# Order of work in a fused two-block transformer kernel: modulation sums, first transfers and one feed-forward seam

## The reference, cut to what matters

```python
# first block
mod = silu(c) @ w_ada + b_ada                     # 1024 -> 6 x 1024
shift1, scale1, gate1, shift2, scale2, gate2 = split(mod, 6)
h = rms_norm(x, g_norm1) * (1 + scale1) + shift1
proj = h @ w_in                                   # and so on: attention, w_out, w_up, w_down
# second block, layer 0
mem_n = rms_norm(mem, mem_norm_g)                 # a memory of 256 rows
mkv   = mem_n @ a_mem_kv                          # keys and values; layer 1 has b_mem_kv
...
x = x + concat([y_mix, m]) @ a_w_out              # "a_out" in the kernel
x = x + swiglu(rms_norm(x, a_norm2_g), a_ffn_gu, a_ffn_down)    # "a_gu", "a_down"
```

## Time and profile before

| | |
|---|---|
| median of 3 runs | 1088.08 us (1087.13 to 1091.59) |
| the profiled execution | 1086.01 us, of it span 1084.2 us |
| PE busy | 1037.8 us (96% of the span) |
| DVE busy | 740.6 us (68%) |
| ACT busy | 553.7 us (51%) |
| DMA | 185.88 MB, mean 171 GB/s |

### The profile page before, as it was taken

One profiled execution on the slowest core, in us unless ns is written; L12 is line 12 of the kernel. 1 busy time (PEld: TensorE's weight loads), 2 busy tenths in 40 slices (PEclk: granted clock), 3 DMA queues, 4 the chain that ended last, 5 costly groups with the idle time before them and its releaser, 6 DMA issues.

```text
span 1084.2 us, 23734 instructions
## 1 busy us (share of the span) xinstructions
PE 1037.8 (96%) x10388; PEld 986.5 (91%) x10388; DVE 740.6 (68%) x1216; ACT 553.7 (51%) x836; POOL 0.9 (0%) x7
## 2 busy tenths in 40 slices
PE   7999999899999999999798999999999999999996
PEld 6888889899999998886678999999998799999996
DVE  4799758799976667888456555566757755566554
ACT  5426354666556458755135444444667655444531
POOL 0000000000000000000000000000000000000000
PEclk8999999999999999999999999999999999999998
DMA  9958455466645653331004555456323445554451
GB/s 370 382 191 310 177 207 194 156 234 233 233 141 185 221 224 117 118 117 44 5 2 156 195 194 190 139 165 211 129 77 115 183 152 187 184 181 154 168 177 40
DMA packets 30664, 185.88 MB, mean 171 GB/s; under 512 B 3408, under 2 KB 4704, under 8 KB 13408
## 3 DMA queue, kind: packets, MB, share of 16 engines
q1 hardware_dynamic: 30560, 184.36, 47.1%
HBM read 183.29 MB, written 1.05 MB: 170 GB/s over the span
## 4 chain that ended last, share of the span: by engine, by line
PE 88%; DVE 6%; ACT 3%; DMA 1%; issue 1%; SPq 0%; DVEq 0%; ACTq 0%
PE banks L359 47%; PE banks L1338 17%; PE banks L339 5%; PE banks L356 2%; DVE wlo L319 1%; PE banks L630 1%; ACT whi L304 1%; PE banks L633 1%; DMA raw<-in_ada 1%; PE banks L568 1%; PE banks L1860 1%; PE banks L1877 1%; PE banks L1870 1%; PE banks L1522 1%; DVE adac L552 1%
## 5 line engine op out<-in xcount | busy, mean ns | idle before, releaser
L319 DVE TENSOR_TENSOR wlo<-raw,whi 128x2048 fp32r<-128x2048 f32 (+3 forms) x163 | 323.1, 1983 | 173.6 <-ACT whi L304 172.8
L304 ACT ACTIVATE whi<-raw 128x2048 fp32r<-128x2048 f32 (+3 forms) x163 | 270.7, 1662 | 121.6 <-PE banks L1338 76.8
L359 PE MATMUL banks<-h_hi,whi 128*128 128x256 f32 x1376 | 182.7, 284 | 1.3 <-ACT h_hi L980 1.2
L359 PE MATMUL banks<-h_lo,whi 128*128 128x256 f32 x1376 | 178.5, 281 | 0.7 <-DVE h_lo L1052 0.7
L359 PE MATMUL banks<-h_hi,wlo 128*128 128x256 f32 x1376 | 178.3, 281 | 0.0
L359 PEld LDWEIGHTS banks<-h_hi,whi 128*128 128x128 f32 x1376 | 170.4, 190 | 5.1 <-issue 2.8
L359 PEld LDWEIGHTS banks<-h_lo,whi 128*128 128x128 f32 x1376 | 167.2, 187 | 3.5 <-issue 1.8
L359 PEld LDWEIGHTS banks<-h_hi,wlo 128*128 128x128 f32 x1376 | 168.5, 189 | 1.5 <-issue 1.0
L1364 ACT ACTIVATE u<-u 128x256 f32<-128x256 f32 x44 | 18.4, 418 | 128.9 <-DVE u L1418 128.8
L1338 PE MATMUL banks<-m_lo,whi 128*128 128x256 f32 x528 | 75.0, 280 | 0.0
L1338 PE MATMUL banks<-m_hi,whi 128*128 128x256 f32 x528 | 74.9, 280 | 0.0
(11 more groups left out here) (448 smaller groups left out, 1394.0 us busy)
## 6 DMA issues: line engine op xcount, KB each, us to landing
raw<-in_ada SPq DMA_DIRECT2D x24, 1024.0 KB, 5.3
raw<-in_w_up SPq DMA_DIRECT2D x22, 1024.0 KB, 4.8
raw<-in_a_gu SPq DMA_DIRECT2D x22, 1024.0 KB, 4.8
raw<-in_b_gu SPq DMA_DIRECT2D x22, 1024.0 KB, 4.8
raw<-in_w_in SPq DMA_DIRECT2D x12, 1024.0 KB, 6.1
raw<-in_w_down SPq DMA_DIRECT2D x16, 704.0 KB, 4.1
raw<-in_a_in SPq DMA_DIRECT2D x11, 1024.0 KB, 5.6
raw<-in_a_down SPq DMA_DIRECT2D x16, 704.0 KB, 4.1
```

Source lines behind the costliest of these rows:

```text
L304: act.activation(hi_s[k % NSPLIT][:, 0:w], raw[n % NRAW][:, 0:w], ACT.Copy).then_inc(*hi_made.tick(k))
L319: dve.tensor_tensor(lo_s[s][:, 0:w], raw[n % NRAW][:, 0:w], hi_s[s][:, 0:w].bitcast(F), SUB).then_inc(*lo_made.tick(k))
L359: i_ = pe.matmul(b[0:m, j * T:(j + 1) * T], a[:, kt * step + j * m:kt * step + j * m + m], x[:, kt, :], start=st, stop=sp)
```

## The change

In the prologue: `mem` and the first memory weights are each loaded by one transfer instead of two halves, and the first memory product goes through its sixteen products by output half, with one wait for its weights. The second memory weights are issued ahead of X instead of behind it. PE's sums of modulation chunks stand one to three pieces later among the memory products, so do the two means with the column; the sums of 6 and 7 stand together ahead of the last piece. `pe_wake` runs seven products instead of five.

At the seam: ScalarE and VectorE make the splits of `a_gu` 0 and 1 ahead of squares 2 and 3 or between them, squares 4 to 7 come behind the gains, and the split of `a_gu` 2 is last on both.

```diff
-        d_mem, d_wfg = [sig(f"landed_mem{i}", 16) for i in range(2)], sig("landed_wfg", 16)
-        d_mkv = [[sig(f"landed_mkv{i}_{n}", 16) for n in range(2 if i == 0 else 1)] for i in range(4)]
+        d_mem, d_wfg = sig("landed_mem", 16), sig("landed_wfg", 16)
+        d_mkv = [sig(f"landed_mkv{i}", 16) for i in range(4)]
...
         def act_mem_gain(act):
             for kt in range(8):
-                if kt % 4 == 0:
-                    act.wait_ge(*d_mem[kt // 4].at(0))
...
             w, b = mkv_w[c], bank[c % 2]
-            halves = [range(0, 4), range(4, 8)] if c == 0 else [range(8)]
-            turns = [(n, j, kt) for n, half in enumerate(halves) for j in range(2) for kt in half]
-            for o, (n, j, kt) in enumerate(turns):
-                if j == 0 and kt == halves[n][0]:
-                    pe.wait_ge(*d_mkv[c][n].at(0))
+            pe.wait_ge(*d_mkv[c].at(0))
+            for o, (j, kt) in enumerate(itertools.product(range(2), range(8))):
...
             act.preload_act_table_set(LN_EXP)
+            act.wait_ge(*d_mem.at(0))
             act_mem_gain(act)
...
-        EARLY_SUMS = {(0, 2): 0, (1, 0): 1, (1, 3): 2, (2, 1): 3, (2, 3): 4, (3, 0): 5, (3, 2): 6, (3, 3): 7}
+        EARLY_SUMS = {(0, 3): (0,), (1, 1): (1,), (2, 0): (2,), (2, 2): (3,), (3, 0): (4,), (3, 1): (5,), (3, 2): (6, 7)}
...
-            if c == 0 and piece == 3:
+            if c == 1 and piece == 0:
                 pe.wait_ge(*d_con0.at(0))
                 pe_mean8(pe, "mem", bank[5])
-            if c == 1 and piece == 1:
+            if c == 1 and piece == 3:
                 pe_mean8(pe, "n1", bank[6])
                 pe_rs_column(pe)
-            if (c, piece) in EARLY_SUMS:
-                pe_ada(pe, EARLY_SUMS[c, piece])
+            for i in EARLY_SUMS.get((c, piece), ()):
+                pe_ada(pe, i)
...
-            for n in range(5):
+            for n in range(7):
                 pe.matmul(bank[0][:, 0:T], rmask[:, 0:P], rmask[:, 0:T], start=True, stop=True)
...
         def act_residual_a(act):
-            for f in range(6):
-                act.wait_ge(*x_made.at(("a_out", f)))
-                act_square(act, "a_out", f, X[:, f, :])
+            def squares(*fs):
+                for f in fs:
+                    act.wait_ge(*x_made.at(("a_out", f)))
+                    act_square(act, "a_out", f, X[:, f, :])
+
+            squares(0, 1)
             act_split(act, split_k["a_out", 1] + 3)
             act_split(act, split_k["a_out", 2] + 3)
+            squares(2, 3)
             act.wait_ge(*done_at("a_out", 3))
             for kt in range(8):
                 act_gain1(act, "nf2", kt, X, V("a_g2", 0, 8), x_made.at(("a_out", kt)))
-            for f in (6, 7):
-                act.wait_ge(*x_made.at(("a_out", f)))
-                act_square(act, "a_out", f, X[:, f, :])
+            squares(4, 5, 6, 7)
             act_split(act, split_k["a_out", 3] + 3)
...
         def dve_residual_a(dve):
-            for i in range(4):
+            def tiles(i):
                 dve.wait_ge(*done_at("a_out", i))
                 for j in range(2):
                     f = 2 * i + j
                     dve.tensor_tensor(X[:, f, :], res_bank("a_out", i)[:, j * T:j * T + T], X[:, f, :],
                                       ADD).then_inc(*x_made.tick(("a_out", f)))
-                if i == 0:
-                    dve_square(dve, "a_out", 1)
-                if i == 2:
-                    for f in range(2, 6):
-                        dve_square(dve, "a_out", f)
-                    dve_split(dve, split_k["a_out", 1] + 3)
+
+            tiles(0)
+            dve_square(dve, "a_out", 1)
+            tiles(1)
+            tiles(2)
+            dve_split(dve, split_k["a_out", 1] + 3)
+            dve_square(dve, "a_out", 2)
+            dve_square(dve, "a_out", 3)
+            dve_split(dve, split_k["a_out", 2] + 3)
+            tiles(3)
             for kt in range(8):
                 dve_gain1(dve, "nf2", kt, X, V("a_g2", 0, 8))
-            dve_square(dve, "a_out", 6)
-            dve_split(dve, split_k["a_out", 2] + 3)
+            for f in (4, 5, 6):
+                dve_square(dve, "a_out", f)
             dve_split(dve, split_k["a_out", 3] + 3)
...
                 if n == 0:
-                    for h in range(2):
-                        t4, c4 = slice(4 * h, 4 * h + 4), slice(1024 * h, 1024 * h + 1024)
-                        sp.dma_start(mem[:, t4, :], A["memT"][:, t4, :]).then_inc(*d_mem[h].tick(0))
-                        sp.dma_start(mkv_w[0][:, c4], A["mkv_a"][0][:, c4]).then_inc(*d_mkv[0][h].tick(0))
+                    sp.dma_start(mem[:, :, :], A["memT"]).then_inc(*d_mem.tick(0))
+                    sp_mkv(sp, 0)
                 if n == 2:
                     sp.dma_start(con[:, 0:NFIRST], A["cons"][:, 0:NFIRST]).then_inc(*d_con0.tick(0))
+                    sp_mkv(sp, 1)
                     sp.dma_start(X[:, :, :], A["xT"]).then_inc(*d_x.tick(0))
-                    sp_mkv(sp, 1)
```

More of the change, by code:

```diff
@@ L1 @@
+import itertools
 import math
@@ L3200, in sp_mkv @@
             name, i = ONE[c]
-            sp.dma_start(mkv_w[c], A[name][i]).then_inc(*d_mkv[c][0].tick(0))
+            sp.dma_start(mkv_w[c], A[name][i]).then_inc(*d_mkv[c].tick(0))
         def sp_program(sp):
```

## The result

The changed kernel takes 1085.48 us (median of 12 runs, 1082.51 to 1088.76), the kernel before 1088.51 us (12 runs beside it, 1086.71 to 1092.45): ratio 0.9972 [0.9959, 0.9985], so 3.0 us faster, which is less than 0.5%. The forecast was 1084.5 us. In a second set it took 1086.71 us, ratio 0.9984 [0.9968, 1.0]. (A ratio compares runs side by side, so it is not exactly the quotient of the medians.)

A forecast was written before the change was run, and what follows sets the result against it. TensorE, busy 96% of the span, was taken as the bound, so gains come only from its waits or low clock. Prologue 2.1 + seam 1.5 = 3.6 us off the median of 1088.08 gave 1084.5 us, range 1081.8 to 1088.8.

The forecast's parts named there:

- S, the first memory product: Prologue: PE's first memory product starts at 9.8 (ends 9.3 and 10.5), before 7.94, costing PE 1.4 to 2.6 us.
- S + 17.5 to the column: Prologue: PE runs without waiting for sum 0, so VectorE's copy of the column comes at 27.3, before at 28.34.
- From the column 18.1 us to mod (16.9 + 1.2): Prologue: VectorE works 16.9 us to chunk 7's end, then 1.2 to its mod row: 45.4 if the clock holds.
- this cap: Prologue: arrival of modulation weights allows mod at 45.2 at old rates, so DMA caps the gain at about 4 us.
- The clock falls at the start and costs 1.65, mod at 47.1: Prologue, forecast case: PE idles 2.8 us before the first memory product and the clock falls; chance 0.46.
- clock holds: Rival, prologue start: idle may be the old 1.80 us; gain 3.8 + 1.5, so 1082.8 us; chance 0.22.
- The rule weighed there: Prologue start: the skill says idle gaps over about 3 us drop the clock; at the seam 2.78 us was enough.
- The gain at mod: 2.1: Prologue: VectorE's mod at 47.1 instead of 49.18, a gain of 2.1 us.
- The seam: 0.69 us, then 2.0 us of new wait, gain 1.5: From a_out to a_gu: PE starts 2.1 us sooner, then waits 2.0 for square 6; means at 587.3, before 588.86.
- The chance of 0.45 for a fall in the new wait: Seam: PE's new wait ahead of the means may drop the clock in any case, adding 1.65 us; chance 0.45.
- The total: Whole kernel: 2.1 + 1.5 = 3.6 us gained, giving 1084.5 us.
- I count what mod gains as kept: After the prologue: w_in steps start from mod or a weight slot they free, so mod's gain is kept.

The follow-up runs named there:

- halves: The changed kernel with mem and the first memory weights loaded in halves again, first product in half-turns: 1088.71 us, ratio to before 0.9987.
- prologue only: The changed kernel with the seam's order of before (old residual functions): 1086.26 us, ratio to the kernel before 0.9964.
- wake of five: The changed kernel with five products of ones in pe_wake instead of seven: 1087.06 us, ratio to the kernel before 0.9977.
- X first: The changed kernel with X issued ahead of the second memory weights again: 1089.03 us, ratio to the kernel before 0.9999.
- after: The whole changed kernel against the kernel before: 1085.48 us, ratio 0.9972; in a second set 1086.71 us, 0.9984.
- seam once more: Repeat of the kernel before with the seam's new order alone: 1088.59 us, ratio to the kernel before 1.0002.
- means covered: The changed kernel with the second feed-forward's means behind two of six pieces of a_gu chunk 1: 1082.77 us, ratio to before 0.9946.
- seam only: The kernel before with the new order of the seam alone: 1088.87 us, ratio to the kernel before 1.0002.
- ones at the seam: The kernel before with six unused products of ones behind chunk 3 of a_out: 1088.59 us, ratio to the kernel before 0.9989.
- Both covered: The changed kernel with second and third feed-forwards' means both behind two of six pieces of chunk 1: 1083.88 us, ratio to before 0.9961.

## Why the prediction was right, and where it was not

- *S, the first memory product.* Forecast 9.8, no sooner than 9.3; measured 8.59. Mis-sized: I let the transfers gain only what lies between 335 and 423 GB/s over 2.1 MB (1.2 us). All three windows from 3.00 on became faster, and chunk 0 behind them landed at 11.06 where it was 13.04, 2.0 us sooner. The halves undo it (249 to 311 GB/s). And 7.94 was an early start: the other three profiles with the old transfers and five products have 8.56, 8.72 and 8.51, so the 1.4 to 2.6 us that whole transfers were to cost PE are not there. The Trainium skill (DMA: Bandwidth & Descriptors, Rules for kernel authors) asks for 1 MiB or more in one DMA for the most bandwidth. The trace agrees: halves of 0.52 MB moved at 249 to 311 GB/s with the queues 85 to 101% busy, wholes of 1.05 MB at 355 to 424. Size and length of the rows changed together, and no run tells them apart.
- *S + 17.5 to the column.* Measured 26.02 - 8.59 = 17.4, with no wait for sum 0. Right to 0.1 us.
- *From the column 18.1 us to mod (16.9 + 1.2).* Right as a term, and not what decided. Where the column is late (prologue only, wake of five, halves, X first), mod minus column is 18.03 or 18.04 all four times, with no wait of VectorE but the last 1.15 us. With the column at 26.02 this gives 44.05, and arrival of chunk 6, with the low clock in sum 7, gives 45.03 (44.7 without). The forecast had this cap, as 45.2, but put it behind the clock's case instead of beside it. It did not have PE's wait for the third weights.
- *The clock falls at the start and costs 1.65, mod at 47.1.* This step failed in both halves. In after, it did not fall (the rival "clock holds"); seven products leave it up in 7 of 8 profiles. And where it does fall, the column is 1.4 us later, but in after mod lies 1.0 above the column's bound, so it loses only 0.43 to 0.48. A loss on PE was priced as though nothing were waiting beside it.
- *The rule weighed there.* The Trainium skill (TensorE: Matmul & The Clock Gate, Why this matters for your kernels) warns of idle gaps of over about 3 us. By that rule the clock would hold at the start, and in after it did, behind 1.31 us of idle. But it fell behind 1.99 us (prologue only), 2.62 (wake of five) and 1.76 (seam once more), and held behind 2.34 (means covered). The measurements decide: in this kernel no length of the gap alone tells the two apart. Before's profile had shown this already, in a row that I did not weigh; the granted clock is 0.50 from 50.6 to 57.4:

```profile
50.39 5.64 PE L359 MATMUL banks<-h_hi,whi 128*128 128x256 f32 x16 [1.25 <-ACT h_hi L980]
```

- *The gain at mod: 2.1.* Profile against profile, 4.15. But before's profile was a late one: three more executions with the old prologue (seam only, once more, and ones at the seam) have mod at 48.41, 47.47 and 47.71, with 49.18 a mean of 48.19. Five executions with the new prologue have 45.03, 45.24, 45.46, 44.97 and 45.39, a mean of 45.22. The prologue is thus worth 3.0 us, and its medians agree: 0.9964 for the prologue alone (3.9 us, interval 2.0 to 5.9), 0.9971 for its transfers alone (3.2 us).
- *The seam: 0.69 us, then 2.0 us of new wait, gain 1.5.* Measured 0.69, 1.76 and 1.6. Right at the place. The chance of 0.45 for a fall in the new wait: 2 of 8 profiles (wake of five, and seam once more), while the old order fell in all 3 profiles that have its idle unfilled. That would leave 1.2 us on average, and two medians say 1.0002, whose intervals reach down to 0.999 and 0.9982, so up to 1.1 and 1.9 us. Whether the seam gives 1 us or nothing stays open.
- *The total.* 3.6 forecast, 3.0 measured, and 1.7 in the second set (0.9984). That the number is near is in part luck: two errors cancel, as far as the medians tell. The prologue brings 3.0 rather than 2.1, the seam somewhere between nothing and 1 rather than 1.5. "I count what mod gains as kept" holds on average, but can't be seen in one span, which scatters by 2 to 3 us behind 127.
- *The versions with covered means.* The means covered have the lowest median and the lowest ratio. 2.0 us of that are shown at the place; the rest of the 4 us below after in its set is more than any view explains. Both covered, which takes away the same wait and no other, has 0.9961, not below the prologue's own 0.9964, and the intervals of all three overlap. So a gain over the prologue alone is not shown by medians.

## What to carry to other kernels

Where the first transfers fill the queues, their size and their order can decide the prologue (here the two together are shown, each alone by one profile): send them whole, and in the order in which the bottleneck needs them, before touching the order of the work. When two chains meet at one instruction, write both as bounds and take the later one; a loss on the other chain costs only what exceeds the distance between them. Moving work ahead of another moves a wait too: look at once for what is released last afterwards (here the means), and whether the next stage has products that can stand in front of it.

## What the hardware showed that was not expected

- The same queues, as busy, moved 249 to 311 GB/s in halves (4 KB rows) and 355 to 424 in wholes (8 KB rows), from the first window on.
- The granted clock fell behind idles of 0.97 us (after, at 44), 1.25 (before, at 50.6) and 1.76 to 3.24 us and held behind others of up to 2.34 us, and the same instruction order had both outcomes: seam only held, once more fell, each with 1.76 or 1.77 us of idle. Low stretches lasted about 3.5 or about 7 us, and some places have one in every profile. What decides was not found.
- PE at times stood for up to 1.6 us with no releaser ("issue") in a layer of short instructions, differently in each execution. What causes it was not tried.
